# Rotary and mix chunks in one stage, rotation stores in four pieces, square sums earlier on ScalarE

## What is computed

```python
h = rmsnorm(x, g)
z = einsum('bsd,de->bse', h, w_in)                 # 1024 -> 4096 features
q, k, v, g_attn, c_h, c_b, c_c, g_conv = split(z)  # 768 x4, then 256 x4
q, k = rope(q), rope(k)                            # t1*cos - t2*sin, t2*cos + t1*sin
attn = dilated_window_attn(q, k, v) * silu(g_attn)
conv = c_b * causal_depthwise_conv(c_c * c_h, conv_w) * silu(g_conv)   # 3 taps
x = x + rmsnorm(concat(attn, conv) @ w_out, g_post)
```

## Time and profile before

| | us |
|---|---|
| median of 3 runs | 2259.65 |
| lowest and highest run | 2259.04, 2260.92 |
| the profiled execution, its time | 2263.17 |
| its span from first to last instruction | 2261.3 |
| TensorE busy | 2024.0 |
| VectorE busy | 1524.7 |
| ScalarE busy | 980.3 |
| GpSimd busy | 982.8 |

### The profile page before, as it was taken

The page is one execution under the profiler, slowest core; times in us unless marked ns, Lnnn a source line. Parts: engine busy times, 40 slices in busy tenths (PEclk is TensorE's granted clock), DMA queues, the critical chain, the costliest instruction groups (busy, mean ns, idle before and its releaser), DMA issues.

```text
span 2261.3 us, 43932 instructions
## 1 busy us (share of the span) xinstructions
PE 2024.0 (90%) x16552; PEld 1498.2 (66%) x16552; DVE 1524.7 (67%) x3562; ACT 980.3 (43%) x2117; POOL 982.8 (43%) x1064
## 2 busy tenths in 40 slices
PE   5999999996888999698899986899989888787998
PEld 3545868886887887587744433345977777665886
DVE  7615949765996556778656776454399999995422
ACT  4323334222884011332433443233189999882111
POOL 4312333363434998433332231434033888974222
PEclk9999999998999999899999998899999999998999
DMA  5441321346632242422232221122467888674552
GB/s 183 140 118 54 111 73 45 96 145 200 154 91 100 93 154 107 140 95 67 66 103 75 64 86 51 43 75 68 95 137 163 203 201 194 167 207 140 165 172 87
DMA packets 272977, 267.38 MB, mean 118 GB/s; under 512 B 35344, under 2 KB 224656, under 8 KB 272512
## 3 DMA queue, kind: packets, MB, share of 16 engines
q1 hardware_dynamic: 268720, 258.48, 40.2%
q0 software_dynamic: 1680, 5.51, 0.7%
q10 hardware_dynamic: 2368, 0.60, 0.1%
HBM read 171.22 MB, written 93.31 MB: 117 GB/s over the span
## 4 chain that ended last, share of the span: by engine, by line
PE 26%; DVE 23%; POOL 11%; DMA 7%; issue 6%; ACT 3%; SPq 0%; DVEq 0%; ACTq 0%; POOLq 0%
PE bank L445 12%; PE bank L3104 7%; DVE s2m L2953 5%; DVE p2l L2959 4%; PE bank L173 3%; DMA scr_k2l<-qt 2%; DMA scr_q2l<-qt 2%; POOL xr L2008 2%; POOL xr L1995 2%; POOL xr L1993 2%; POOL xr L2010 1%; PE bank L1637 1%; DVE xl L851 1%; DVE qt L2247 1%; DVE qx L2209 1%
## 5 line engine op out<-in xcount | busy, mean ns | idle before, releaser
L173 PE MATMUL bank<-w1h,xh 128*128 128x256 f16 x768 | 210.7, 274 | 3.0 <-DVE s1st L1169 3.0
L173 PE MATMUL bank<-w1l,xh 128*128 128x256 f16 x768 | 210.6, 274 | 0.0
L173 PE MATMUL bank<-w1h,xl 128*128 128x256 f16 x768 | 210.5, 274 | 0.0
L2898 PE MATMUL bank<-ident,p2r 128*128 128x128 f32 x900 | 165.8, 297 | 49.6 <-DVE p2l L2959 42.9
L445 PE MATMUL bank<-xh,w2h 128*128 128x512 f16 x320 | 126.9, 397 | 45.8 <-DVE u L2356 22.9
L2898 PEld LDWEIGHTS bank<-ident,p2r 128*128 128x128 f32 x900 | 97.5, 145 | 106.0 <-DVE p2l L2959 103.3
L2959 DVE SCALAR_TENSOR_TENSOR p2l<-bank,p2h 128x512 f16<-128x512 f32 (+1 forms) x288 | 163.6, 568 | 3.0 <-ACT p2h L2925 2.8
L1179 DVE SCALAR_TENSOR_TENSOR bank<-ain,cw,bank 128x512 f32<-128x512 f32 x208 | 157.0, 755 | 8.0 <-ACT bank L1124 1.7
L2953 DVE CUSTOM_DVE_ANT_0 s2m<-bank,both,finv 128x256 f32<-128x256 f32 (+1 forms) x384 | 160.2, 454 | 0.0
L173 PE MATMUL bank<-w2h,xh 128*128 128x256 f16 x512 | 143.2, 280 | 14.5 <-DVE xl L851 13.5
L2932 ACT ACTIVATE p2r<-s2m,ob 128x128 f32<-128x128 f32 (+1 forms) x384 | 147.5, 436 | 13.1 <-DVE ob L2953 12.7
(11 more groups left out here) (457 smaller groups left out, 6361.1 us busy)
## 6 DMA issues: line engine op xcount, KB each, us to landing
scr_part<-ob SPq DMA_DIRECT2D x48, 264.0 KB, 2.7
cm<-scr_part SPq DMA_DIRECT2D x48, 264.0 KB, 4.6
v<-scr_v SPq DMA_DIRECT2D x192, 65.0 KB, 2.7
ax<-in_x SPq DMA_DIRECT2D x16, 512.0 KB, 5.7
xr<-in_x SPq DMA_DIRECT2D x16, 512.0 KB, 4.5
bx<-scr_x SPq DMA_DIRECT2D x16, 512.0 KB, 7.7
x2r<-scr_x SPq DMA_DIRECT2D x16, 512.0 KB, 4.3
out<-yo SPq DMA_DIRECT2D x16, 512.0 KB, 2.9
```

The source lines that it names most:

```text
L173: ins = nc.tensor.matmul(dst, x, y, start=k == 0 and m == 0, stop=k == n - 1 and m == 2)
L2898: ins = nc.tensor.transpose(bank[:, w * hh + 128 * c:w * hh + 128 * c + 128], p[:, hh, 128 * c:128 * c + 128], ident[:])
```

## The change

- `rope_stage` and `mix_stage` become `rope_mix_stage`: one work list over 20 pairs (`ROPE` = 12 of them rotary), with no hand-over between. Their buffers share one area, `room`: the mix part's buffers lie where the sine and cosine tables, `qx` and `qt` lie in the rotary part. New waits guard that: the first mix sums wait for the last rotary ones (`d_rp`, `d_u`), `acc` and `tbuf` for `d_ql`, `hbuf` and `lbuf` for all rotation stores (`stored`).
- Each rotation store becomes four DMAs, one for each head: 32 partitions to 32 rows.
- After the joint stage ScalarE and VectorE wait for everything but the stores of the mix outputs, GpSimd and SyncE for everything.
- In `norm_stage` chunk 3's squares are taken in four operations into a PSUM bank (`spread`), `("load", 3)` moves up behind `("split", 2)`, and `("total", 3)`, `("scaled", 3)`, `("load", 4)` and `("total", 4)` move up against their neighbours.

```diff
-    def wait_all(new):
-        for eng in (act, dve, pool, sp):
+    def wait_all(new, engines=None):
+        for eng in engines or (act, dve, pool, sp):
...
-            work += [("cast", 0, "T2"), ("split", 2), ("pair", 0, "T4"), ("cast", 0, "T4"), ("group", 1, 3), ("tail", 0, "T2"),
-                     ("pair", 0, "T3"), ("cast", 0, "T3"), ("load", 3), ("tail", 0, "T4"), ("group", 2, 1), ("total", 3), ("tail", 0, "T3"),
-                     ("pair", 1, "T1"), ("scaled", 3), ("group", 2, 3), ("pair", 1, "T2"), ("cast", 1, "T2"), ("group", 2, 0), ("load", 4),
-                     ("pair", 1, "T4"), ("cast", 1, "T4"), ("tail", 1, "T2"), ("total", 4), ("group", 2, 2), ("scaled", 4), ("tail", 1, "T4"),
+            work += [("cast", 0, "T2"), ("split", 2), ("load", 3), ("pair", 0, "T4"), ("cast", 0, "T4"), ("group", 1, 3), ("tail", 0, "T2"),
+                     ("pair", 0, "T3"), ("total", 3), ("cast", 0, "T3"), ("tail", 0, "T4"), ("group", 2, 1), ("tail", 0, "T3"), ("scaled", 3),
+                     ("pair", 1, "T1"), ("group", 2, 3), ("load", 4), ("pair", 1, "T2"), ("cast", 1, "T2"), ("group", 2, 0), ("total", 4),
+                     ("pair", 1, "T4"), ("cast", 1, "T4"), ("tail", 1, "T2"), ("group", 2, 2), ("scaled", 4), ("tail", 1, "T4"),
...
-    def rope_stage(scope, wts, first, xs, xs_ready, fits):
+    def rope_mix_stage(scope, wts, first, xs, xs_ready, fits):
 
         begin()
+        ROPE, ALL = 12, 20
...
+        room = sb("rm", [128, 10752], scope=scope)
+        cosT, sinT = room[:, 0:2048], room[:, 2048:4096]
+        qx, qt = [room[:, at:at + 1024] for at in (4096, 5120, 6144)], [room[:, at:at + 1024] for at in (7168, 8192)]
+        m1, u2, u4 = ([room[:, at:at + 512], room[:, 512 * k:512 * k + 512]] for k, at in enumerate((9216, 9728, 10240)))
+        uin, acc = room[:, 1536:1536 + S + 2], room[:, 3600:3600 + S]
...
+        work = slots_of(ALL // 2, ("out",), lambda i, q: TURNS[q] if i < ROPE else ((1, "times"), (2, "tail"), (3, "last")), PREPARE + [(12, "fit")])
...
+        stored = [s.at(64 * ROPE) for s in (*h_out, *l_out)]
...
-            dst = ((q2h, q2l), (k2h, k2l))[n // 3][m].rearrange("(n h t e) s -> n t h e s", h=4, t=2, e=32)
-            return nc.sync.dma_start(dst[n % 3, step][:, :, 1024 * P:1024 * P + 1024], qt[step][:].bitcast(FH)[:, 1024 * m:1024 * m + 1024])
+            dst, r = ((q2h, q2l), (k2h, k2l))[n // 3][m], 256 * (n % 3) + 32 * step
+            for h in range(4):
+                nc.sync.dma_start(dst[r + 64 * h:r + 64 * h + 32, 1024 * P:1024 * P + 1024],
+                                  qt[step].bitcast(FH)[32 * h:32 * h + 32, 1024 * m:1024 * m + 1024]).then_inc(*done.up(16))
...
+                    else:
+                        act.wait_ge(*wts.scaled[first + i // 2])
+                        act.wait_ge(*(d_u.at(5 * ROPE - 1) if i == ROPE else d_rp.at(6 * ROPE)))
...
+                    if i >= ROPE:
+                        dve.wait_ge(*(d_u.at(5 * ROPE) if i == ROPE else d_rp.at(6 * ROPE)))
...
-    chunks2 += [chunk("n", [(G2, 256)])]
+    chunks2 += [chunk("n", [(G2, 256)], spread=True)]
...
-            rope_stage(s2, wts, 4, xs, xs_ready, fits)
-            wait_all(hand_over())
-        with stack() as s2:
-            mix_stage(s2, wts, 10, xs)
-            wait_all(hand_over())
+            stores = rope_mix_stage(s2, wts, 4, xs, xs_ready, fits)
+            done = hand_over()
+            wait_all(done, (pool, sp))
+            wait_all([x for x in done if x[0] not in stores], (act, dve))
```

More of the change, by code:

```diff
@@ L198, in __init__ @@
             done = 0 if first is None else 1
-            by_parts = [c["seven"] for c in chunks]
+            by_parts = [c["spread"] for c in chunks]
             self.summed = [(self.a_n, self.a_n.n + n + 1 - done + 3 * sum(by_parts[:n + 1])) for n in range(len(chunks))]
@@ L272, in pe_total @@
             pe.wait_ge(*before)
-            own, k = (self.parts_[:, n, :], 4) if self.chunks[n]["seven"] else (self.size[:, n, 0:1], 1)
+            own, k = (self.parts_[:, n, :], 4) if self.chunks[n]["spread"] else (self.size[:, n, 0:1], 1)
             nc.tensor.matmul(bank[:, 0:k], ones_[:], own, start=True, stop=True).then_inc(*self.p_t.up())
@@ L552, in norm_stage @@
                 made[item] = d_tl.at(n_tail)
-            elif item[0] == "load" and item[1] > 3:
+            elif item[0] == "load" and item[1] > 2 and late:
                 junk_bank[item[1]] = bk.take(wts.summed[item[1]])
@@ L2092, in slots_of @@
                 work += [(x, *done) for x in outs]
-                for later, what in after(done[1]):
+                for later, what in after(*done):
                     due.setdefault(at + later, []).append((what, *done))
@@ L2176, in pe_program, with act_mix @@
                     wts.pe_total(first + item[1] + 2, *total_bank[first + item[1] + 2])
+        def act_mix(what, i, q):
+            _, _, P, j = of(i)
+            if what == "out" and q in (0, 3):
+                b = q // 3
+                act.wait_ge(*d_m.at(6 * (i - ROPE) + 3 * b + 3))
+                act.wait_ge(*d_bl.at(2 * j - 1 + b))
+                act.wait_ge(*d_ql.at(2 * ROPE))
+                nc.scalar.activation(tbuf[b], (u4, u2)[b][P], ACT.Tanh, scale=0.5).then_inc(*a_th.up())
+            elif what == "tail" and q in (2, 3):
+                b = q - 2
+                act.wait_ge(*d_bs.at(4 * j + 2 + 2 * b))
+                act.wait_ge(*h2_out[b].at(16 * j))
+                for s in stored:
+                    act.wait_ge(*s)
+                nc.scalar.activation(hbuf[b], tbuf[b], ACT.Copy).then_inc(*a_bh.up())
         def act_program():
@@ L2194, in act_program @@
                     nc.scalar.activation(half(i, step, 0), whole(i, step), ACT.Copy).then_inc(*a_qh.up())
+                elif item[0] in ("out", "tail") and not of(item[1])[0]:
+                    act_mix(*item)
                 elif item[0] == "sum":
@@ new lines, in dve_rope @@
+        def dve_rope(what, i):
+            c = slice(1024 * (i % 2), 1024 * (i % 2) + 1024)
+            if what in ("cross_low", "cross_high"):
+                step = int(what == "cross_low")
+                if step:
+                    dve.wait_ge(*c_in.at(80))
+                    dve.wait_ge(*a_q.at(i + 1))
+                dve.wait_ge(*d_u.at(5 * i + (4 if step else 5)))
+                dve.wait_ge(*h_out[step].at(64 * i))
+                dve.wait_ge(*l_out[step].at(64 * i))
+                dve_turn(qt[step], (low if step else high)(i), sinT[:, c], ALU.mult)
+            elif what == "high":
+                dve_turn(high(i), high(i), cosT[:, c], ALU.mult)
+                dve_turn(high(i), high(i), qt[1], ALU.add)
+            elif what == "low":
+                dve_turn(low(i), low(i), cosT[:, c], ALU.mult)
+            elif what == "low_add":
+                dve_turn(low(i), low(i), qt[0], ALU.subtract)
+            elif what in ("high_lo", "low_lo"):
+                step = int(what == "high_lo")
+                dve.wait_ge(*a_qh.at(2 * i + 2 - step))
+                nc.vector.tensor_tensor(half(i, step, 1), whole(i, step), half(i, step, 0), ALU.subtract).then_inc(*d_ql.up())
@@ new lines, in dve_conv @@
+        def dve_conv(i, c, P):
+            at, n = 1024 * P, 1024 * P + 1024
+            dve.wait_ge(*mul_at(i, 3))
+            dve.wait_ge(*d_z.now())
+            dve.wait_ge(*REST)
+            dve.wait_ge(*d_ql.at(2 * ROPE))
+            nc.vector.tensor_scalar(acc[:, at:n], uin[:, at:n], cw2[:, c, 0:1], None, ALU.mult).then_inc(*d_cv.up())
+            for m in range(1, 3):
+                dve.wait_ge(*d_cv.now())
+                nc.vector.scalar_tensor_tensor(acc[:, at:n], uin[:, at + m:n + m], cw2[:, c, m:m + 1], acc[:, at:n], ALU.mult, ALU.add).then_inc(*d_cv.up())
@@ new lines, in dve_mix @@
+        def dve_mix(what, i, q):
+            conv, c, P, j = of(i)
+            if conv:
+                if what == "tail" and q == 3:
+                    dve_conv(i, c, P)
+                return
+            if what == "times" and q in (0, 3):
+                b = q // 3
+                dve.wait_ge(*a_th.at(2 * j + 1 + b))
+                nc.vector.scalar_tensor_tensor(tbuf[b], tbuf[b], 1.0, (u4, u2)[b][P], ALU.add, ALU.mult).then_inc(*d_bs.up())
+            if (what, q) in (("tail", 2), ("times", 3)):
+                b = q - 2
+                s = 1024 * P + 512 * (1 - b)
+                if b == 0:
+                    dve.wait_ge(*mul_at(i, 2))
+                dve.wait_ge(*d_bs.now())
+                nc.vector.scalar_tensor_tensor(tbuf[b], tbuf[b], 0.5, acc[:, s:s + 512], ALU.mult, ALU.mult).then_inc(*d_bs.up())
+            if what == "last" and q in (2, 3):
+                b = q - 2
+                dve.wait_ge(*a_bh.at(2 * j + 1 + b))
+                dve.wait_ge(*l2_out[b].at(16 * j))
+                for s in stored:
+                    dve.wait_ge(*s)
```

(14 more changed lines are left out.)

311 lines of the change are left out of this document (92 added, 219 removed).

## The result

The changed kernel takes 2198.0 us (median of 4 runs, 2193.7 to 2201.1) against 2260.0 for the kernel before in the same session (2259.0 to 2260.9): a ratio of 0.9724, 95% interval 0.9706 to 0.9743, so 62 us or 2.8% faster. The forecast was 2176.9 with a range of 2171 to 2205: the time is inside it, and 21 us above the point. The profiled execution is the fastest of the four (2193.72, span 2191.9).

What follows compares the result with a forecast made beforehand. TensorE, busy 90%, was taken to lose time to stalls on late stores and square sums and the slow clock after them; 33.2 + 25.5 + 7.2 + 19.4, less 2.5 kept, gave 82.8 us saved: 2176.9 us, range 2171 to 2205.

Steps and rivals of the forecast that it cites:

- Issue and landing of the pieces: Rotation stores: four pieces take 0.45 us each to issue; the last lands about 4.3 us after the trigger.
- Store waits go: Rotary stage: no VectorE wait over 1 us on `scr_q2l` or `scr_k2l`, where store waits totalled 42.8 us.
- part 4: Border to the gate stage: skipping the last `c2h` and `c2l` stores' wait saves 4.4 us stall and 2.8 clock, 7.2.
- The rest behind the border: After the rotary-to-mix border: 2.6 us of slow clock behind its stall and 7.2 at the gate stage go.
- part 5: Norm stage: earlier square sums remove stalls of 7.8 and 6.0 us plus clock, 19.4 in all, 0.5 kept.
- B: Norm stage keeps a stall, or its gain is lost before chunk 4 is ready: +9 to +19 us; chance 0.10.
- C: Rotation stores get no faster, pieces running one after the other: +38 us, 2215; chance 0.05.
- D: SyncE's queue becomes the bound in the rotary stage: 2338 us at 2.0 us per piece; chance 0.03.
- part 2: VectorE in rotary pairs: work fits without store waits; critical piece 7.4 us against TensorE's 7.8; 33.2 us gained.
- Rival A: VectorE becomes the bound in even rotary pairs: six stalls of 1 to 3 us, middle 2197 us; chance 0.17.
- 2.0 kept for thin margins: Even rotary pairs: 2.0 us of loss left standing in the sum, bounds 0 and 20.
- list of what the profile should show: Signs from rotary to gate stage: no TensorE wait over 3 us, 20 pairs in 362 to 368 us, PEclk 1.00.

Runs made afterwards that it cites:

- experiment 7: The changed kernel, with ScalarE and VectorE again waiting for every store at the border to the gate stage: 2206.6 us.
- experiment 8: The kernel before, with only the norm stage's edits (chunk 3's squares in four parts, items moved up): 2239.0 us, ratio 0.9899 to the kernel before.
- experiment 3: The changed kernel, with the old norm stage order and chunk 3's squares in one operation again: 2220.9 us, ratio 0.9827 to the kernel before.
- experiment 4: The changed kernel, with GpSimd's A22 and A splits moved into the odd pair for chunks 5 and later: 2174.9 us, ratio 0.9628 to the kernel before.
- experiment 6: The changed kernel, with GpSimd's A22 and A splits in the odd pair and also, with nobody waiting, at their old place: 2197.5 us.

## Why the prediction was right, and where it was 21 us too low

**Right, with their sizes.** *Issue and landing of the pieces*: 0.45 each and about 4.3 us to the last landing were forecast; 0.43 came, and about 3 x 0.43 + 1.7 = 3.0, since the time to landing counts from the start of a piece's issue. *Store waits go*: 1.1 and 0.7 us are left. *Border to the gate stage* (part 4): 7.2 forecast, 7.2 in experiment 7. *The rest behind the border*: 9.8 forecast (2.6 + 7.2), 9.5 came. *Norm stage* (part 5): 18.9 forecast, 19.8 by the trace, 21.8 and 22.9 in experiments 8 and 3; part of what is more in the two experiments is pair 0's wait of 1.9, which the prediction left in place for the hand-over; it goes with the new norm order alone (experiment 8) and is back with the old one (experiment 3). The other rivals are out: no square sum stalls (B), pieces land fast (C), SyncE's queue doesn't bind (D). The 2.0 us per DMA that D takes from the Trainium skill, DMA: Bandwidth & Descriptors, stands there in the section "Anatomy of one DMA — SWDGE (gpsimd) path", which is about DMAs issued by GpSimd; these are SyncE's, and no run shows 2.0 per piece in series.

**The step that failed** is the critical piece in part 2: "from `cross_high`'s start to `u2`'s end 6.32". The 6.32 was read in a stretch where GpSimd's A22 and A splits had just ended, because VectorE had been waiting for the store while they ran. With that wait removed the same VectorE instructions start beside them and take 9.25: 7.4 + 2.9 = 10.3 against TensorE's 7.8, a stall of 2.5 by this sum and 2.35 measured, instead of a margin of 0.4. Rival A, with its chance of 0.17, is what came: it named six stalls of 1 to 3 us and 2197. So the time lies in the range because the range took in most of A, not because the forecast's own mechanism held. A's mechanism was only half right. It thought of VectorE's total (17.9 of 18.1 us); what binds is this one piece, and freeing it alone (experiment 4) removes all six stalls though VectorE's work stays.

In numbers: rotary stage and border together were to gain 33.2 + 22.9 - 2.0 = 54.1 and gained 35.6. The stretch at full clock takes 225.5 us; it took 248.0, so 22.5 is lost: 14.1 in six stalls and 8.4 besides: four dips of the clock of about 1.7 are 6.8, and 1.6 isn't placed. The forecast had left 3.9 (pair 0's 1.9 and the 2.0 kept). The 2.0 kept for thin margins (bounds 0 and 20) is the term that was mis-sized: it has to carry the whole 22.5, since pair 0 no longer stalls. Experiment 4, 0.9628 against 0.9724, gives 21.7 us of it back, and its 2174.9 is 2.0 us from the forecast that assumed no such stalls.

Some of the distance is which execution is compared. The sum gave 2180.4 for the profiled execution, which took 2193.7, 13.3 us more; the other 7.8 are the 3.5 by which the prediction went down from the profiled execution to the median, and the 4.3 by which the profiled execution of the changed kernel lies below its own. Of the 69.4 gained in the profile 4.5 lie where nothing was changed, and are luck as far as any run shows. One number of the prediction doesn't follow from its sum: with nothing kept the forecast would be 2174.4, not 2172.

Of the list of what the profile should show, three points fell with this: 20 pairs took 386 us (362 to 368 forecast), PEclk wasn't 1.00 throughout, and TensorE waits for `rm` in even pairs. Two more were off by themselves: one VectorE wait of 1.1 us on `scr_q2l` where none over 1 was to be, and a DMA share of 0.55 where nearly 1 was forecast. "No wait over 3 us" held.

**Not settled**: why the clock falls after some stalls of 2.35 us and not after others. That the runs' spread comes from it fits (7.4 us with the stalls, 3.3 without; a mean clock of 0.975 in the fastest run and 0.970 or 0.971 in the others; four falls in the execution of 2193.7 us, five in one of 2201.7), and was not tested by itself.

## What to carry to other kernels

A duration read next to a wait is a duration under that wait's protection. Before a wait is removed, lay the other engines' timelines over it: what ran while this engine stood still will now run beside it, and here VectorE's operations with two SBUF inputs and GpSimd's took turns. A wait's removal is then worth its full price only together with a move of that work (here: the move alone 0, the rest alone 2.8%, both 3.7%). And look at a transfer's outermost dimension before its size: four pieces of 32 rows beat one store of four heads, and two pieces of two heads lose to both.

## What the runs showed of the hardware that was not expected

- Two-input operations on VectorE and GpSimd alternate as wholes: 0.68 us became 2.61, 1.23 became 2.22. The slower number appears under VectorE's line, and GpSimd's own split stretches from 2.12 to 3.11; nothing in the waits names it.
- When stores of two heads queue up, the issue itself slows down: SyncE spends 0.48 us on the first of a group and up to 5.8 us on a later one, so the queue that issues is held as well. The Trainium skill, Perfetto Trace Analysis, section "DMA Instruction — HWDGE (DVE, Sync)", describes a descriptor buffer that fills before all descriptors are generated; that fits, and no run here isolates it.
- The lower clock follows stalls as short as 2.35 us in four cases of six (five of six in the execution of experiment 6), at about 1.7 us each; the prediction had counted it only for stalls of 3 us and more.
